# Up-projection of a split-precision feed-forward stage: two of the three products merged into one 512-column product

## The chip, the core and the metric

One core of a Trainium2 chip. The metric is the device time of one execution in microseconds, the median of several. The kernel computes a whole four-layer network in one launch.

## The reference

The network has two transformer layers (differential attention, then latent attention), each followed by the same convolution-gated feed-forward and a per-layer embedding, then two more mixers. Width is 1024, sequence 256, all in float32. What the change touches is this, once per layer of the first two:

```python
def conv_gated_ffn(h, w_in, conv_w, conv_b, w_out):      # h: 256 x 1024, w_in: 1024 x 5632, w_out: 2816 x 1024
    u = h @ w_in                                         # the up-projection
    u_pad = jnp.pad(u, ((0, 0), (CONV_WIDTH - 1, 0), (0, 0)))
    c = conv_b
    for j in range(CONV_WIDTH):                          # 3 taps along the sequence
        c = c + u_pad[:, j:j + s, :] * conv_w[j]
    a, g = jnp.split(c, 2, axis=-1)
    return (jax.nn.silu(g) * a) @ w_out
```

`h` is RMS-normalised first; its gain is folded into `x`, and the row factor 1/rms is applied when the product leaves PSUM.

## The kernel before

**Precision.** Every float32 operand of a product is split in two fp32r parts, high and low. `mm3` (L412 to L415) makes three products of one weight tile: high weight by high x (L413), high weight by low x (L414), low weight by high x (L415), all summed in the same PSUM bank. In the feed-forward the weight tile of 128x128 is the stationary operand and x, 256 tokens wide, streams past it.

**The weight stream.** All weights come as 295 panels of eight 128x128 tiles, in the order of use. SyncE loads a panel into one of six RAW buffers (L380) once its previous content was split. ScalarE (ACT) writes the high part WH (`split_hi`, L1817), which waits until TensorE (PE) has used the panel three before (`w_used`); VectorE (DVE) writes the low part WL (`split_lo`, L1123) after it. There are three WH/WL slots. PE waits for both parts (`take`, L408).

**One feed-forward stage** (`ffn(layer)` on PE L760, DVE L1452, ACT L2006, GpSimd L2420) has 66 panels and 22 hidden tiles j. Hidden tile j has 128 channels of a and 128 of g. Its turn on PE: `hidden` (L765), two panels, eight weight tiles each (one per 128 features of x), a into columns 0 to 255 of a PSUM bank G0 or G1 and g into columns 256 to 511; the banks alternate with j. Then `down` (L776), one panel: the finished hidden tile j-2 times w_out, summed over all j in the four banks A0 to A3. Tile 0 is special (L786 to L795): it goes to a G bank and A3, and its last two k wait for the last parts of x; after it come four small products for the sum of squares (`row_stats`), then tile 1, and turns 2 to 21; at the end two more `down` panels for hidden tiles 20 and 21. After some turns PE makes modulator products for later (L547).

**Around a turn**, the other engines run in a written-out order:
- DVE (`turn`, L1488): split_lo of the next turn's first panel; the eviction `tile` (L1466, one 128x512 operation that multiplies both halves by the row factor, writes U and frees the bank); split_lo; `conv` (two taps, L1473 and L1478, four operations); split_lo.
- ACT (`turn`, L2036): split_hi, split_hi, `conv` (third tap and bias, L2021, two operations, reads U), split_hi, `gate` (Silu, L2027).
- GpSimd (`hidden`, L2423): product of the gated halves twice (L2428, L2429) and its low part (L2432), which lets `down` run.

The panel splits of a turn wait, by w_used, for the panel in the same place of the turn before: the third for `down` of the current turn. ACT's order at the start (L2009 to L2034): splits, `root` of the row sum (L1827), split, split, conv(0), gate(0), split, conv(1), gate(1). DVE's (L1481 to L1486): reciprocal of the row factor (L1138), splits, then tile, split and conv for tiles 0 and 1. In layer 1 DVE also has a second reciprocal in turn 2 and four operations of another branch (L1436) in each of turns 3 and 4, and in both layers one low part for the embedding (L1501) after turn 5.

`UNITS` (L58) counts how often G0 and G1 are evicted in all; the wait counts for a bank come from it (u0).

## Time and profile before

| | us |
|---|---|
| median of 3 executions | 1317.41 (1317.01 to 1320.32) |
| the profiled execution's own time | 1318.33 |
| its span, first to last instruction | 1316.6 |
| mean granted TensorE clock | 0.997 |
| feed-forward stage of layer 0, in the span | from about 173 to 378 |
| feed-forward stage of layer 1 | from about 593 to 798 |

The profile is one execution as the hardware profiler recorded it. PE is TensorE's matmuls, PEld its weight loads, DVE VectorE, ACT ScalarE, POOL GpSimd. In a timeline a row has start and length of an instruction in us; [0.91 <-DVE WL L1123] says that the engine sat idle 0.91 us until DVE's instruction of line 1123 on WL was done; x2 says that two like instructions were merged. Tile names are those of the underlying buffers: U is in ATT, the convolution's result in ATT and HSQ, the gate's in HRS. A matmul's length holds its latency, so the pitch between starts is what it costs.

### The profile page before, as it was taken

Reading aid. Unit: us, or ns where it says so; the run is one execution under the profiler, and the core shown is the slowest. Engines: PE = TensorE matmul, PEld = TensorE weight load, DVE = VectorE, ACT = ScalarE, POOL = GpSimd, SP = SyncE. Lnnn points to the kernel's source line nnn. Section 1 sums busy time; section 2 is a strip of 40 time slices with the busy share of each in tenths; the row PEclk is TensorE's granted clock in tenths of the full one; section 3 lists DMA queues with packets and bytes.
Section 4 is the critical chain, followed back from the end, with each engine's and each line's share of the span. In section 5 each row is a group of like instructions: output and inputs, shape, how many; then the busy total and the mean of one; then the engine's idle time right before and its main releaser. Section 6 shows DMA issues by size and latency. Waiting matters only on the chain.

```text
span 1316.6 us, 24170 instructions
## 1 busy us (share of the span) xinstructions
PE 1259.6 (96%) x8884; PEld 1089.8 (83%) x8884; DVE 883.2 (67%) x1388; ACT 689.6 (52%) x1217; POOL 364.9 (28%) x377
## 2 busy tenths in 40 slices
PE   6999999999999999999999999999989999999996
PEld 4887899999998877898999998888755699987666
DVE  6878588666768985558976667753377548453674
ACT  5555455444567777545554447544367515413562
POOL 4942145344321140144444332011012220000022
PEclk9999999999999999999999999999999999999998
DMA  8565247566545532255665664422200364522100
GB/s 311 178 219 193 65 144 263 202 237 237 198 144 175 165 124 96 67 190 173 228 227 208 236 206 135 134 73 95 95 1 1 71 170 144 160 97 80 49 1 33
DMA packets 50361, 191.72 MB, mean 146 GB/s; under 512 B 5792, under 2 KB 6048, under 8 KB 47968
## 3 DMA queue, kind: packets, MB, share of 16 engines
q1 hardware_dynamic: 43488, 158.59, 36.5%
q0 software_dynamic: 6064, 31.33, 6.8%
q8 instruction: 62, 1.02, 0.3%
q10 hardware_dynamic: 720, 0.57, 0.2%
q14 instruction: 27, 0.22, 0.1%
HBM read 189.41 MB, written 1.05 MB: 145 GB/s over the span
## 4 chain that ended last, share of the span: by engine, by line
PE 78%; DVE 9%; ACT 7%; issue 3%; DMA 1%; POOL 1%; SPq 0%; DVEq 0%; ACTq 0%; POOLq 0%
PE G L413 14%; PE G L415 13%; PE G L414 13%; PE A L413 6%; PE A L415 6%; PE A L414 6%; DVE WL L1123 3%; PE R L633 3%; PE R L559 2%; ACT WH L1817 2%; PE A L991 1%; PE R L413 1%; PE R L415 1%; PE R L414 1%; PE G L1000 1%
## 5 line engine op out<-in xcount | busy, mean ns | idle before, releaser
L1123 DVE TENSOR_TENSOR WL<-RAW,WH 128x1024 fp32r<-128x1024 f32 x295 | 382.2, 1302 | 291.8 <-ACT WH L1817 291.4
L1817 ACT ACTIVATE WH<-RAW 128x1024 fp32r<-128x1024 f32 x295 | 310.4, 1057 | 415.1 <-PE G L415 302.7
L413 PE MATMUL G<-XH,WH 128*128 128x256 f32 (+1 forms) x1336 | 400.1, 299 | 9.6 <-DVE WL L1123 6.3
L414 PE MATMUL G<-XL,WH 128*128 128x256 f32 (+1 forms) x1336 | 394.9, 296 | 0.0
L415 PE MATMUL G<-XH,WL 128*128 128x256 f32 (+1 forms) x1336 | 394.9, 296 | 0.0
L413 PEld LDWEIGHTS G<-XH,WH 128*128 128x128 f32 x1336 | 255.3, 191 | 33.2 <-issue 25.8
L414 PEld LDWEIGHTS G<-XL,WH 128*128 128x128 f32 x1336 | 255.5, 191 | 6.3
L415 PEld LDWEIGHTS G<-XH,WL 128*128 128x128 f32 x1336 | 255.5, 191 | 6.3
L413 PE MATMUL A<-HH,WH 128*128 128x256 f32 x352 | 99.8, 283 | 3.7 <-POOL HL L2432 3.7
L414 PE MATMUL A<-HL,WH 128*128 128x256 f32 x352 | 99.6, 283 | 0.0
L415 PE MATMUL A<-HH,WL 128*128 128x256 f32 x352 | 99.5, 283 | 0.0
L2408 POOL CAST XH<-HRS 128x256 fp32r<-128x256 f32 x24 | 11.4, 474 | 267.3 <-DVE HRS L1714 267.3
L1204 DVE TENSOR_REDUCE SM<-A 128x2 f32<-128x1024 f32 (+1 forms) x80 | 67.8, 849 | 17.9 <-PE A L991 12.9
L413 PEld LDWEIGHTS A<-HH,WH 128*128 128x128 f32 x352 | 67.6, 192 | 4.1 <-ACT WH L1817 4.1
L2428 POOL TENSOR_TENSOR HRS<-HSQ,HRS 128x256 f32<-128x256 f32 x22 | 32.0, 1456 | 128.6 <-ACT HRS L2027 128.6
L415 PEld LDWEIGHTS A<-HH,WL 128*128 128x128 f32 x352 | 67.6, 192 | 0.0
L414 PEld LDWEIGHTS A<-HL,WH 128*128 128x128 f32 x352 | 67.6, 192 | 0.0
L1856 ACT ACTIVATE ATT<-R 128x1024 f32<-128x1024 f32 (+3 forms) x56 | 37.7, 674 | 56.9 <-PE R L633 56.9
L413 PE MATMUL G<-WH,XH 128*128 128x512 f32 (+1 forms) x136 | 54.8, 403 | 12.5 <-DVE XL L1149 11.1
L2428 POOL TENSOR_TENSOR HRS<-ATT,HRS 128x256 f32<-128x256 f32 x22 | 32.1, 1457 | 98.1 <-ACT HRS L2027 92.6
L413 PE MATMUL A<-WH,XH 128*128 128x512 f32 x144 | 57.3, 398 | 1.5 <-DVE XL L1444 1.3
L415 PE MATMUL A<-WH,XL 128*128 128x512 f32 x144 | 56.2, 390 | 0.0
(345 smaller groups left out, 2364.7 us busy)
## 6 DMA issues: line engine op xcount, KB each, us to landing
RAW<-in_wst SPq DMA_DIRECT2D x295, 512.0 KB, 3.8
M<-in_wmod POOLq DMA_DIRECT2D x16, 1024.0 KB, 6.6
M<-in_wmod POOLq DMA_DIRECT2D x16, 512.0 KB, 6.3
B<-in_rpb POOLq DMA_DIRECT2D x4, 1024.0 KB, 12.0
H<-in_x_t SPq DMA_DIRECT2D x2, 512.0 KB, 8.3
M<-in_x_tok SPq DMA_DIRECT2D x1, 1024.0 KB, 13.4
M<-in_ctx_t POOLq DMA_DIRECT2D x1, 1024.0 KB, 5.1
out_y<-M SPq DMA_DIRECT2D x2, 384.0 KB, 2.7
```

Of the source, the lines that this page charges most:

```text
L413: mm(out, lh, rh, start=start, stop=False, skip_group_check=True)
L414: mm(out, lh, rl, start=False, stop=False, skip_group_check=True)
L415: return mm(out, ll, rh, start=False, stop=stop, skip_group_check=True)
L559: m = mm(O[32 * g:32 * g + 32, q * P:(q + 1) * P], SC[:, k, :], RN[:, i % RMS, k * P:(k + 1) * P], start=(k == 0), stop=(k == KD - 1), ski ...
L633: m = nc.tensor.transpose(ST[c][:, k * P:(k + 1) * P], PRB[a % 3][:, c, k * P:(k + 1) * P], IDT)
L991: m = mm(out[c][:, 0:nk * P], Q2[64 * c:64 * c + 64, t, qt * P:(qt + 1) * P], K2[64 * c:64 * c + 64, t // 4, k0:512], start=True, stop=Tru ...
L1000: m = mm(out[64 * c:64 * c + 64, 0:T], V2[:, k + (0 if nk == 4 else 2), kv * 64:(kv + 1) * 64], pt[:, c, k, :], start=(k == 0), stop=(k == ...
L1123: v.tensor_tensor(WL[:, slot, :], RAW[:, raw, :], WH[:, slot, :].bitcast(F32), ALU.subtract).then_inc(w_lo, 1)
L1204: v.tensor_reduce(small(80, a, 2), sc, AX, ALU.max, negate=True).then_inc(at_mx, 1)
L1817: act(WH[:, slot, :], RAW[:, raw, :], ACT.Copy).then_inc(w_hi, 1)
L1856: act(att(s, j)[:, 0:width, 0:nk, q * P:(q + 1) * P], RO[:, :].rearrange("p (l k q) -> p l k q", l=2, k=4)[:, 0:width, 0:nk, :], ACT.Copy) ...
L2428: g.tensor_tensor(HID[b], CB[b][:, 0, :], SG[b], ALU.mult).then_inc(f_hid, 1)
```

## The change

The up-projection makes two products of a weight tile instead of three. XH and XL become halves of one buffer XX, and the high weight tile multiplies both in one product of 512 columns: columns 0 to 255 of the bank get high weight by high x, 256 to 511 high weight by low x. The low weight tile by high x is added to columns 0 to 255. So a bank now holds one of a and g, and the two halves have to be added when it is evicted. ACT copies the right half to LO (in HSQ), DVE adds the left half to it into U, and when both a and g are there DVE multiplies U by the row factor in place. Tile j uses G0 for a and G1 for g; tile 0 uses A2 and A3. `down` and all other stages keep three products.

The order on ACT in a turn becomes: split_hi, copy of a's low half, gate of the tile before, split_hi, copy of g's low half, split_hi, conv. On DVE: split_lo, add a, split_lo, add g, scale, split_lo, conv. At the start ACT has: splits, two copies for tile 0, root, split, split, conv(0), gate(0), two copies for tile 1, split, conv(1). The last gate comes after the loop.

```diff
 
-UNITS = [("l0_o", 4), ("ffn0", 22), ("pp0", 4), ("pg0", 4),
-         ("l1_o", 4), ("ffn1", 22), ("pp1", 4), ("pg1", 4),
+UNITS = [("l0_o", 4), ("ffn0", 42), ("pp0", 4), ("pg0", 4),
+         ("l1_o", 4), ("ffn1", 42), ("pp1", 4), ("pg1", 4),
          ("a_z", 8), ("a_o", 8),
...
         WL = sb("WL", [P, SPL, PW], F32R)
-        XH = sb("XH", [P, 16, T], F32R)
-        XL = sb("XL", [P, 16, T], F32R)
+        XX = sb("XX", [P, 2, 16, T], F32R)
+        XH, XL = XX[:, 0, :, :], XX[:, 1, :, :]
         H = sb("H", [P, KD, T])
...
         CB = [UB[:, 1032:1544].rearrange("p (a t) -> p a t", a=2), HSQ[:, 0, :].rearrange("p (a t) -> p a t", a=2)]
+        LO = HSQ[:, 1, :].rearrange("p (a t) -> p a t", a=2)
         SG = [HRS[:, 0, 0:T], HRS[:, 1, 0:T]]
...
         f_zero, bias_ok = sem("f_zero"), sem("bias_ok")
+        f_low, f_sum, f_u = sem("f_low"), sem("f_sum"), sem("f_u")
         p_hi, p_lo, p_sg, p_m = sem("p_hi"), sem("p_lo"), sem("p_sg"), sem("p_m")
...
 
-                def hidden(par, pslot, bslot, free, p):
+                def both(out, wh, wl, k):
+                    mm(out.rearrange("p (a t) -> p a t", a=2), wh, XX[:, :, k, :], start=(k == 0), stop=False, skip_group_check=True)
+                    return mm(out[:, 0:T], wl, XH[:, k, :], start=False, stop=(k == KD - 1), skip_group_check=True)
+                def hidden(pslot, free, p):
 
-                    pe.wait_ge(bank_free[bslot], free)
                     for c in range(2):
+                        pe.wait_ge(bank_free[c], free)
                         take(p + c)
...
                             wh, wl = wtile((pslot + c) % SPL, k)
-                            m = mm3(G[bslot][:, c * T:(c + 1) * T], wh, wl, XH[:, k, :], XL[:, k, :],
-                                    k == 0, k == KD - 1)
+                            m = both(G[c][:, :], wh, wl, k)
                         m.then_inc(w_used, 1)
...
 
-                pe.wait_ge(bank_free[u0 % 2], u0 // 2)
                 for ks in (range(6), range(6, KD)):
...
                             wh, wl = wtile((p0 + c) % SPL, k)
-                            m = mm3((A[3] if c else G[u0 % 2])[:, 0:T], wh, wl, XH[:, k, :], XL[:, k, :], k == 0, k == KD - 1)
+                            m = both(A[2 + c], wh, wl, k)
                         if k == KD - 1:
...
                 row_stats(tag)
-                hidden(1, p0 + 2, (u0 + 1) % 2, (u0 + 1) // 2, p0 + 2)
+                hidden(p0 + 2, u0 // 2, p0 + 2)
                 def tile(j, i=0):
...
                     q = p0 + 4 + 3 * (j - 2)
-                    hidden(j % 2, q, (u0 + j) % 2, i * 2 + (u0 + j) // 2, i * 12 + q)
+                    hidden(q, i * 4 + (u0 // 2 + j - 1), i * 12 + q)
                     down(j % 2, q + 2, i * 4 + (hb + j - 1), i * 12 + (q + 2), j == 2, False)
...
 
-                def tile(b, bslot, j, p, n):
+                def added(b, c, n):
 
-                    dv.wait_ge(w_used, p)
-                    if isinstance(j, int) and j == 0:
-                        v.tensor_tensor(U[b][:, 0, 2:2 + T], G[bslot][:, 0:T], RST[:, 0, :], ALU.mult)
-                        v.tensor_tensor(U[b][:, 1, 2:2 + T], A[3][:, 0:T], RST[:, 0, :], ALU.mult).then_inc(bank_free[bslot], 1)
-                        return
-                    v.tensor_tensor(U[b][:, :, 2:2 + T], G[bslot][:, :].rearrange("p (a t) -> p a t", a=2),
-                                    bc(RST[:, 0, :], 2), ALU.mult).then_inc(bank_free[bslot], 1)
+                    dv.wait_ge(f_low, 2 * n + c + 1)
+                    v.tensor_tensor(U[b][:, c, 2:2 + T], G[c][:, 0:T], LO[:, c, :], ALU.add).then_inc(bank_free[c], 1)
+                def scaled_by(b, freed):
+                    for c in range(2):
+                        dv.wait_ge(bank_free[c], freed)
+                    v.tensor_tensor(U[b][:, :, 2:2 + T], U[b][:, :, 2:2 + T], bc(RST[:, 0, :], 2), ALU.mult).then_inc(f_u, 1)
 
...
                 ahead(p0 + 2)
-                for j in range(2):
-                    tile(j, (u0 + j) % 2, j, p0 + 2 * j + 2, hb + j)
-                    ahead(p0 + 3 + j)
-                    conv(j, j, hb + j)
+                for c in range(2):
+                    dv.wait_ge(f_low, 2 * hb + c + 1)
+                    v.tensor_tensor(U[0][:, c, 2:2 + T], A[2 + c][:, 0:T], LO[:, c, :], ALU.add).then_inc(f_sum, 1)
+                dv.wait_ge(f_sum, 2 * layer + 2)
+                v.tensor_tensor(U[0][:, :, 2:2 + T], U[0][:, :, 2:2 + T], bc(RST[:, 0, :], 2), ALU.mult).then_inc(f_u, 1)
+                ahead(p0 + 3)
+                conv(0, 0, hb)
+                for c in range(2):
+                    added(1, c, hb + 1)
+                scaled_by(1, u0 // 2 + 1)
+                ahead(p0 + 4)
+                conv(1, 1, hb + 1)
 
-                def turn(b, bslot, j, p, s, r, n):
+                def turn(b, freed, j, p, s, r, n):
 
                     split_lo(p + 3, s % SPL, (r + 0) % RAWS)
-                    tile(b, bslot, j, p + 2, n)
+                    added(b, 0, n)
                     split_lo(p + 4, (s + 1) % SPL, (r + 1) % RAWS)
-                    conv(b, j, n)
+                    added(b, 1, n)
+                    scaled_by(b, freed)
                     split_lo(p + 5, (s + 2) % SPL, (r + 2) % RAWS)
+                    conv(b, j, n)
 
...
                     p = p0 + 4 + 3 * (j - 2)
-                    turn(j % 2, (u0 + j) % 2, j, p, p + 3, p + 3, hb + j)
+                    turn(j % 2, u0 // 2 + j, j, p, p + 3, p + 3, hb + j)
                     if j == 5:
...
                         p = p0 + 16 + 3 * d
-                        turn(d % 2, (u0 + d) % 2, i * 4 + (6 + d), i * 12 + p, p + 3, p + 3, i * 4 + (hb + 6 + d))
+                        turn(d % 2, i * 4 + (u0 // 2 + 6 + d), i * 4 + (6 + d), i * 12 + p, p + 3, p + 3, i * 4 + (hb + 6 + d))
                 nxt[0] = p0 + 67
...
                 p0, u0, hb = START[tag], U0[tag], FT * layer
+                def low(c, bank, p):
+                    ac.wait_ge(w_used, p)
+                    act(LO[:, c, :], bank[:, T:2 * T], ACT.Copy).then_inc(f_low, 1)
                 ahead(p0 + 1)
+                for c in range(2):
+                    low(c, A[2 + c], p0 + c + 1)
                 root(tag, 0, D)
...
 
-                def conv(b, bslot, freed, j, n):
+                def conv(b, j, n):
 
-                    ac.wait_ge(bank_free[bslot], freed)
+                    ac.wait_ge(f_u, n + 1)
                     if not isinstance(n, int) or n >= 2:
...
                 ahead(p0 + 3)
-                conv(0, u0 % 2, u0 // 2 + 1, 0, hb)
+                conv(0, 0, hb)
                 gate(0, hb)
+                for c in range(2):
+                    low(c, G[c], p0 + 3 + c)
                 ahead(p0 + 4)
-                conv(1, (u0 + 1) % 2, (u0 + 1) // 2 + 1, 1, hb + 1)
-                gate(1, hb + 1)
+                conv(1, 1, hb + 1)
 
-                def turn(b, bslot, freed, j, p, s, lands, n):
+                def turn(b, j, p, s, lands, n):
                     split_hi(p + 3, s % SPL, s % RAWS, lands[0])
+                    low(0, G[0], p + 1)
+                    gate(1 - b, n - 1)
                     split_hi(p + 4, (s + 1) % SPL, (s + 1) % RAWS, lands[1])
-                    conv(b, bslot, freed, j, n)
+                    low(1, G[1], p + 2)
                     split_hi(p + 5, (s + 2) % SPL, (s + 2) % RAWS, lands[2])
-                    gate(b, n)
+                    conv(b, j, n)
 
...
                     p = p0 + 4 + 3 * (j - 2)
-                    turn(j % 2, (u0 + j) % 2, (u0 + j) // 2 + 1, j, p, p + 3, lands(p), hb + j)
+                    turn(j % 2, j, p, p + 3, lands(p), hb + j)
                     if j == 4:
...
                         p = p0 + 16 + 3 * d
-                        turn(d % 2, (u0 + d) % 2, i * 2 + ((u0 + 6 + d) // 2 + 1), i * 4 + (6 + d), i * 12 + p, p + 3,
-                             [i * 32 + x for x in lands(p)], i * 4 + (hb + 6 + d))
+                        turn(d % 2, i * 4 + (6 + d), i * 12 + p, p + 3, [i * 32 + x for x in lands(p)], i * 4 + (hb + 6 + d))
+                gate(1, hb + FT - 1)
                 nxt[0] = p0 + 67
```

## Rows read from the trace of the kernel before

**Rows 1.** The page, busy time, share of the span and instructions of each engine.

```profile
PE 1259.6 (96%) x8884; PEld 1089.8 (83%) x8884; DVE 883.2 (67%) x1388; ACT 689.6 (52%) x1217; POOL 364.9 (28%) x377
```

**Rows 2.** The page, chain that ended last, by engine.

```profile
PE 78%; DVE 9%; ACT 7%; issue 3%; DMA 1%; POOL 1%; SPq 0%; DVEq 0%; ACTq 0%; POOLq 0%
```

**Rows 3.** Timeline of PE, layer 0: start us, us, engine, line, operation, out<-in.

```profile
290.39 0.28 PE L413 MATMUL G<-XH,WH 128*128 128x256 f32 x1
...
291.83 0.28 PE L413 MATMUL G<-XH,WH 128*128 128x256 f32 x1
```

**Rows 4.** Timeline of PE, a stage with 512-column products.

```profile
1049.80 0.39 PE L413 MATMUL G<-XH,WH 128*128 128x512 f32 x1
...
1051.84 0.39 PE L413 MATMUL G<-XH,WH 128*128 128x512 f32 x1
```

**Rows 5.** Timeline of PE, start of layer 0's feed-forward stage.

```profile
184.74 0.36 PE L413 MATMUL G<-XH,WH 128*128 128x256 f32 x1 [0.91 <-DVE WL L1123]
...
197.04 0.36 PE L413 MATMUL G<-XH,WH 128*128 128x256 f32 x1 [0.56 <-DVE WL L1123]
```

**Rows 6.** Timeline of PE, last down-projection of layer 0.

```profile
375.60 0.36 PE L413 MATMUL A<-HH,WH 128*128 128x256 f32 x1 [1.86 <-POOL HL L2432]
```

**Rows 7.** Groups of instructions by line and form: xcount | busy us, mean ns | idle.

```profile
L1123 DVE TENSOR_TENSOR WL<-RAW,WH 128x1024 fp32r<-128x1024 f32 x295 | 382.2, 1302 | 291.8 <-ACT WH L1817 291.4
...
L1856 ACT ACTIVATE ATT<-R 128x256 f32<-128x256 f32 x16 | 6.2, 386 | 13.0 <-PE R L633 13.0
...
L1528 DVE TENSOR_TENSOR ATP<-ATP,B 128x512 f32<-128x512 f32 x8 | 5.5, 686 | 1.4 <-ACT ATP L2102 1.4
...
L1168 DVE TENSOR_TENSOR ATP<-R,CS 128x256 f32<-128x256 f32 x9 | 3.4, 415 | 0.0
```

**Rows 8.** Timeline of DVE, start of layer 0's stage.

```profile
183.37 2.36 DVE L1123 TENSOR_TENSOR WL<-RAW,WH 128x1024 fp32r<-128x1024 f32 x2
...
186.31 1.22 DVE L1123 TENSOR_TENSOR WL<-RAW,WH 128x1024 fp32r<-128x1024 f32 x1
187.55 0.88 DVE L1473 SCALAR_TENSOR_TENSOR ATT<-ATT,V 128x256 f32<-128x256 f32 x2
```

**Rows 9.** Timeline of ACT, start of layer 0's stage.

```profile
186.43 1.09 ACT L2021 ACTIVATE ATT<-ATT,V 128x256 f32<-128x256 f32 x2 [1.45 <-DVE ATT L1464]
187.54 1.28 ACT L2027 ACT_TABLE_LOAD   x1
188.99 0.42 ACT L2027 ACTIVATE HRS<-ATT 128x256 f32<-128x256 f32 x1 [0.17 <-DVE ATT L1478]
```

**Rows 10.** Timeline of DVE, two turns of layer 1 apart.

```profile
632.40 1.21 DVE L1123 TENSOR_TENSOR WL<-RAW,WH 128x1024 fp32r<-128x1024 f32 x1
...
641.28 1.21 DVE L1123 TENSOR_TENSOR WL<-RAW,WH 128x1024 fp32r<-128x1024 f32 x1
```

**Rows 11.** Timeline of ACT, end of layer 0's stage.

```profile
370.90 1.06 ACT L1817 ACTIVATE WH<-RAW 128x1024 fp32r<-128x1024 f32 x1 [0.84 <-PE A L415]
371.87 0.40 ACT L2027 ACTIVATE HRS<-HSQ 128x256 f32<-128x256 f32 x1
```

**Rows 12.** Timeline of POOL, last hidden tile of layer 0.

```profile
372.40 1.48 POOL L2428 TENSOR_TENSOR HRS<-HSQ,HRS 128x256 f32<-128x256 f32 x1 [6.74 <-ACT HRS L2027]
...
374.73 0.73 POOL L2432 TENSOR_TENSOR HL<-HRS,HH 128x256 fp32r<-128x256 f32 x1
```

**Rows 13.** Timeline of POOL, first hidden tile of layer 0.

```profile
191.09 1.54 POOL L2432 TENSOR_TENSOR HL<-HRS,HH 128x256 fp32r<-128x256 f32 x1
```

**Rows 14.** Timeline of PE at the kernel's two ends; granted clock after it (PEclk).

```profile
11.10 0.77 PE L413 MATMUL G<-WH,XH 128*128 128x512 f32 x1 [11.10 <-DVE XL L1149]
...
15.08 0.63 PE L413 MATMUL G<-WH,XH 128*128 128x512 f32 x1
...
1307.04 0.70 PE L468 MATMUL R<-ATP,C 128*128 128x256 f32 x2 [0.59 <-ACT ATP L2327]
...
1309.00:1310.00 1.00, 0.00 (x0) 0.66 0.00 0
```

More of the change, by code:

```diff
@@ L1482, in ffn @@
                 ahead(p0 + 2)
-                for j in range(2):
-                    tile(j, (u0 + j) % 2, j, p0 + 2 * j + 2, hb + j)
-                    ahead(p0 + 3 + j)
-                    conv(j, j, hb + j)
-                def turn(b, bslot, j, p, s, r, n):
+                for c in range(2):
[11 more added lines that the diff above has]
+                def turn(b, freed, j, p, s, r, n):
                     split_lo(p + 3, s % SPL, (r + 0) % RAWS)
-                    tile(b, bslot, j, p + 2, n)
+                    added(b, 0, n)
                     split_lo(p + 4, (s + 1) % SPL, (r + 1) % RAWS)
+                    added(b, 1, n)
+                    scaled_by(b, freed)
+                    split_lo(p + 5, (s + 2) % SPL, (r + 2) % RAWS)
                     conv(b, j, n)
-                    split_lo(p + 5, (s + 2) % SPL, (r + 2) % RAWS)
                 for j in range(2, 6):
                     p = p0 + 4 + 3 * (j - 2)
-                    turn(j % 2, (u0 + j) % 2, j, p, p + 3, p + 3, hb + j)
+                    turn(j % 2, u0 // 2 + j, j, p, p + 3, p + 3, hb + j)
                     if j == 5:
```

## The prediction, made before the changed kernel ran

> **What bounds the kernel now.** I read the page first. TensorE is busy for nearly the whole span and VectorE for two thirds of it [rows 1], and the chain that ended last runs mostly through PE, with little in DVE and ACT [rows 2]. Work taken off PE counts in full, unless something else then comes late. The change touches only the two feed-forward stages, some 205 us each (two up-projection panels and one down-projection panel per hidden tile, 22 tiles per layer), so I read the timeline there.
>
> In the middle of a stage PE never waits. A matmul of 256 columns starts every 0.120 us: twelve steps take 1.44 us [rows 3]. A weight tile of three such products costs 0.360 us, a panel of eight 2.88, a turn (two panels up, one down) 8.64. The 512-column products of another stage start every 0.227 us: nine steps take 2.04 us [rows 4]. At 2.4 GHz the columns alone would take 0.107 and 0.213 us, so each matmul carries 0.0133 us that doesn't depend on its width.
>
> The ends of a stage are different. At its start PE waits 0.91 us for a panel's low part and later 0.56 us [rows 5]; at its end it waits 1.86 us for the last hidden tile [rows 6]. There PE hangs on a chain through ACT, DVE and POOL, and the change lengthens that chain.
>
> **PE's own saving.** Columns stay the same (512 + 256 against 3 x 256), one matmul per weight tile goes. An up-projection tile costs 0.2267 + 0.120 = 0.3467 us, a panel 2.77, a turn 8.43 instead of 8.64: 0.213 saved per turn. Over 44 turns, 704 matmuls x 0.0133 = 9.4 us, if nothing else moved. The Trainium skill (TensorE: Matmul & The Clock Gate, "Back-to-back issue gap") gives 2.5 ns beyond the columns for a warm matmul in isolation; by that the saving would be 1.8 us and the sum below 7.6 us higher. The rows show 13.3 ns in streams with a weight load before each matmul, so I keep the rows' value.
>
> **What the evictions cost.** The low half can't be added to the high half in one DVE instruction as cheaply as before: ACT copies each low half (0.39 us for 128x256 from PSUM, two per tile), DVE adds each half (0.42 each), then scales 128x512 (0.69) as the old eviction did [rows 7]. In the steady turn this is covered. Bank G0 is full 2.77 us into a turn and wanted again at 8.43. Between lie PE's signal (0.2), the panel split ahead of the copy on ACT (1.06), the copy (0.4), and on DVE the split (1.3 [rows 7]) and the add (0.4): free at about 6.2, so 2.2 us to spare. DVE's own work per turn is 3 x 1.3 + 0.84 + 0.69 + 1.76 for four convolution steps (0.88 for two [rows 8]) = 7.2 us, against 8.43. Cover is thinner than before but holds. The root of the row sum now stands behind two copies on ACT, about 0.25 us at each start. DMA queues: SP's waits are on the low splits, which come at most one add later, with six raw buffers ahead, so nothing. POOL's modulation loads wait on PE as before: nothing.
>
> **The start of a stage.** Before, tiles alternated banks; tile 2 found its bank long empty. Now tile 2 needs both banks of tile 1, and their low halves are copied on ACT only after the gate of tile 0. I follow layer 0:
> - Root 0.25 later, so the reciprocal and the two splits at 183.37 [rows 8] move to 183.6. PE resumes the second half of tile 1 at 184.95 instead of 184.74 and is ready for tile 2 at 187.8.
> - DVE ends the splits at 185.9 (183.37 + 2.36 = 185.7 before). Two adds with a pitch of 0.35 and a scale that waits for them end at 187.4. ACT's convolution, 186.43 before, starts there [rows 9]; it ends at 188.5, the table load at 189.9. DVE's split (186.31 before) ends 188.5, its convolution gives the gate its input at 189.95.
> - Gate 189.95 to 190.35 (188.99 before), copy to 190.7, add to 191.15, G0 free: PE starts tile 2 at 191.2 instead of 187.8, a hole of 3.4 us.
> - Tile 3 starts at 191.27 + 8.43 = 199.7, where it was 197.04 [rows 5]. The 0.56 us wait there goes, since panels come early now. Term: +2.65.
>
> **The middle.** Tiles 3 to 20 save 18 x 0.213 = -3.85. In layer 1 DVE carries four more operations in each of two turns, a second reciprocal and one longer split near them: its turns then take 8.88 us with no idle (632.40 to 641.28) [rows 10], and with two adds more about 9.6, against PE's 8.43. Starting 2.2 us ahead, less what the reciprocal took, DVE falls behind: tiles 5 and 6 wait for bank 0 about 1.8 us together. Ends: 0 if the slack holds it, 3.0 if splits meet POOL each time.
>
> **The end of a stage.** Before, the last tile's convolution on ACT stood ahead of the third split; now it stands behind it, and that split waits for the down-projection of the same turn. In layer 0's frame (turn 21 starts at 362.0, that is 8.64 and a signal of 0.24 ahead of the split at 370.90 [rows 11]), that split begins at 370.7, ACT convolution ends 372.7, DVE gives the gate its input at 374.2, gate to 374.7 (before 371.87 to 372.27). POOL follows at 374.8 instead of 372.40. Its three operations took until 375.46, 3.06 us, the first 1.48 because DVE was at work [rows 12]; now DVE is idle then and it should take 0.75, but a later split falls beside the others, and one of them took 1.54 beside a split [rows 13]. So 2.3 to 3.2 us: PE's last down-projection starts at 377.2 to 378.1 instead of 375.60. Term +1.6 to +2.5, I take +2.05, in the middle. PE's hole is 3.7 to 4.6 us.
>
> **Sum without the clock.** Layer 0: 2.65 - 3.85 + 2.05 = +0.85. Layer 1: +0.85 + 1.8 = +2.65. Together +3.5 us; ends +0.8 and +5.6.
>
> **The clock.** The four holes (3.4, 3.4 and twice some 4 us) are longer than any idle of PE in the stages before. After PE's last instruction (from 1307.04, 0.70 us long) the granted clock fell between 1309 and 1310, under 3 us later, to its lower level of 1.2 GHz [rows 14]. At the kernel's start PE idled 11.10 us, and at 15.08 a 512-column matmul still took 0.63 us, 0.39 later [rows 4, 14]: some 4.5 us of work at about half speed, which cost 2.25. So a hole costs 0 if the clock stays and about 2.25 if it falls. The row nearest to a hole (the idle end) says it can fall, nothing says it falls each time: I take half, 1.1 each, +4.5 in all; ends 0 and +9. The Trainium skill, same page, "Why this matters for your kernels", says that idle gaps of this kind between bursts bring the low clock back; by it the sum would lie near the upper end.
>
> The forecast: +3.5 + 4.5 = +8.0. The profiled execution took 1318.33 (span 1316.6), which lies 0.92 above the median, so it would go to 1326.3, and the median 1317.41 to **1325.4 us**.
>
> **The rivals.**
> - The clock holds through all holes: +3.5, 1320.9 (1318.2 to 1323.0). For it: PE idled 1.86 us at the stage's end with no fall. Against: the fall after the last instruction.
> - DVE becomes the bound in every turn. If the splits met POOL each time (about 1.65 us instead of 1.3 [rows 13]), DVE's turn would be 8.2, and with waits between its steps up to 8.9; above 8.43 it decides. 36 turns x 0.45 = 16 more: about 1337. Against: DVE sat idle for 291.8 us in all before its splits [rows 7].
> - Faster: the holes don't open, because bank 0 comes free within 1 us of PE's wish and the last convolution isn't held. That leaves nearly -9.4: 1308. Against: the program order of gate, copies and third split is fixed.
> - The change doesn't do what it says: the wide product, whose two halves now lie 4096 elements apart, costs as much as two of 256 columns. No saving: +3.5 + 9.4 + 4.5, 1335. Against: the wide products of another stage, also in two pieces, run at 0.227.
>
> **How the numbers follow.** Forecast (clock falls in some of the holes) 0.52, clock holds 0.28, DVE bound 0.09, no saving from the wide product 0.06, faster 0.05. The range takes in the low bound of the second case and the high bound of the first (+5.6 + 9.0): 1318.5 to 1332. About 0.3% (4 us) is what a measurement can tell from no change. Of the second case 0.17 falls within that, 0.11 above it. Slower: 0.52 + 0.11 + 0.09 + 0.06 = 0.78; same 0.17; faster 0.05.
>
> **What would show it.** Wide matmuls every 0.227 us in the up-projection; a PE wait of 3.4 us for the add of bank 0 ahead of tile 2 in both layers; waits of about 4 us for POOL before the last down-projection; two waits for the bank in layer 1's tiles 5 and 6; the granted clock under 1 in the slices after the holes. Turns of 8.43 us elsewhere. I'm wrong if PE starts tile 2 by 189, if a steady turn is longer than 8.5, or if the matmul pitch differs.

## The result: slower by 1%, and the profile after

| | before | after |
|---|---|---|
| median of the executions timed in turn, us | 1318.24 | 1332.68 (1331.36 to 1333.53) |
| ratio, 95% interval | | 1.0106 [1.0094, 1.0119] |
| span of the profiled execution, us | 1316.6 | 1330.9 |
| mean granted TensorE clock | 0.997 | 0.992 |
| layer 0, first row-sum product of the stage's start to that after its end | 179.9 to 390.1, 210.2 | 179.1 to 394.9, 215.8 |
| layer 1, the same | 599.8 to 809.9, 210.1 | 604.7 to 824.5, 219.8 |

The forecast was +8.0 us, with a range that ended at 1332; measured were +14.4 and 1332.68. The sign and the places were right, the size was not. All of it lies in the two feed-forward stages: +5.6 in layer 0, +9.7 in layer 1. (These add up to 15.3, since the profiled execution of after reached its first stage 0.8 us earlier.) Between and behind the stages nothing moved.

The page of after, busy time by engine:

```profile
PE 1261.6 (95%) x8180; PEld 1057.5 (79%) x8180; DVE 914.2 (69%) x1474; ACT 715.8 (54%) x1305; POOL 362.0 (27%) x377
```

TensorE issues 704 matmuls fewer than in [rows 1] and is busy for 2.0 us more. Holes are idle time, so they can't explain this: the matmuls themselves took longer than foreseen, by their pitch (the time from one start to the next) or by the clock. Next, who made PE wait (total, times, longest):

```profile
PE A L415 <- POOL HL L2459: 9.8, 2, 4.9
...
PE G L769 <- DVE ATT L1468: 4.7, 3, 3.2
...
PE G L769 <- issue: 3.2, 1, 3.2
```

These are four holes and two shorter waits; the "issue" line is the hole of layer 0, which the profile puts down to nothing. That it is a wait for the same bank as in layer 1 is shown by run 4 below, which removes both. In the timeline of PE (start, length, engine, line, operation, idle before and releaser):

```profile
190.09 0.47 PE L769 MATMUL G<-XX,WH 128*128 128x512 f32 x1 [3.21 <-issue]
...
198.69 0.40 PE L769 MATMUL G<-XX,WH 128*128 128x512 f32 x1
...
207.22 0.40 PE L769 MATMUL G<-XX,WH 128*128 128x512 f32 x1
...
378.13 0.55 PE L415 MATMUL A<-HH,WH 128*128 128x256 f32 x1 [4.92 <-POOL HL L2459]
...
382.75 0.41 PE L415 MATMUL A<-HH,WH 128*128 128x256 f32 x1
382.97 0.41 PE L416 MATMUL A<-HL,WH 128*128 128x256 f32 x1
...
615.67 0.79 PE L769 MATMUL G<-XX,WH 128*128 128x512 f32 x1 [3.16 <-DVE ATT L1468]
...
643.45 0.50 PE L769 MATMUL G<-XX,WH 128*128 128x512 f32 x1 [0.53 <-DVE ATT L1468]
...
653.27 0.50 PE L769 MATMUL G<-XX,WH 128*128 128x512 f32 x1 [1.03 <-DVE ATT L1468]
...
807.35 0.55 PE L415 MATMUL A<-HH,WH 128*128 128x256 f32 x1 [4.91 <-POOL HL L2459]
```

What to see: 3.2 us ahead of tile 2 in both layers; 4.9 us ahead of the last down-projection where [rows 6] had 1.86; tiles 5 and 6 of layer 1 waiting for the bank; a turn of 207.22 - 198.69 = 8.53 us with no wait in it, not 8.43. At 382.75 two matmuls of 256 columns stand 0.22 apart instead of 0.12: the clock. In the next rows each number with (x...) is an engine's busy share of that microsecond, in the order PE, PEld, DVE, ACT, POOL; the number right behind them is the granted clock:

```profile
189.00:190.00 1.00, 0.00 (x0) 0.00 (x0) 0.64 (x3) 1.00 (x4) 0.66 (x1) 1.00 0.67 193
190.00:191.00 1.00, 0.91 (x5) 0.85 (x6) 0.90 (x2) 0.75 (x1) 0.86 (x3) 1.00 0.55 221
...
376.00:377.00 1.00, 0.00 (x0) 0.00 (x0) 1.00 (x1) 0.00 (x0) 0.86 (x2) 0.73 0.11 45
377.00:378.00 1.00, 0.00 (x0) 0.00 (x0) 0.41 (x1) 0.00 (x0) 0.99 (x1) 0.50 0.03 8
...
382.00:383.00 1.00, 1.00 (x7) 1.00 (x7) 0.00 (x0) 0.00 (x0) 0.00 (x0) 0.50 0.00 0
383.00:384.00 1.00, 1.00 (x9) 1.00 (x9) 0.44 (x1) 0.38 (x1) 0.00 (x0) 0.85 0.00 0
...
615.00:616.00 1.00, 0.33 (x1) 0.33 (x2) 0.75 (x2) 1.00 (x3) 1.00 (x2) 0.70 0.87 295
616.00:617.00 1.00, 1.00 (x4) 0.81 (x4) 0.95 (x2) 0.39 (x2) 0.86 (x2) 0.50 0.32 131
```

The clock fell to its lower level (0.50) inside both holes of 4.9 us and in the 3.2 us hole of layer 1, not in that of layer 0. The last down-projection of layer 0 ran at that level nearly to its end: 378.13 to 383.36 is 5.23 us for 24 matmuls that take 2.9 at full clock, 2.33 more.

### The profile page after: what moved, and what is told of

Read it like the earlier page. It is cut to its first block, busy times and chain, and to the rows that moved or that the text cites. A ratio compares the mean times of both kernels' runs of the same rounds, so it can differ in the third digit from the quotient of the medians.

```text
span 1330.9 us, 22994 instructions
## 1 busy us (share of the span) xinstructions
PE 1261.6 (95%) x8180; PEld 1057.5 (79%) x8180; DVE 914.2 (69%) x1474; ACT 715.8 (54%) x1305; POOL 362.0 (27%) x377
## 4 chain that ended last, share of the span: by engine, by line
PE 78%; DVE 9%; ACT 7%; issue 3%; POOL 1%; DMA 1%; SPq 0%; DVEq 0%; ACTq 0%; POOLq 0%
PE G L769 11%; PE G L415 8%; PE G L417 8%; PE G L416 8%; PE A L415 6%; PE A L417 6%; PE A L416 6%; PE G L770 5%; DVE WL L1129 3%; PE R L635 3%; PE R L561 2%; ACT WH L1834 2%; PE R L415 1%; PE R L417 1%; PE R L416 1%
## 5 line engine op out<-in xcount | busy, mean ns | idle before, releaser
L769 PE MATMUL G<-XX,WH 128*128 128x512 f32 x672 | 243.0, 404 | 9.8 <-DVE ATT L1468 4.7
L415 PE MATMUL G<-XX,WH 128*128 128x256 f32 (+1 forms) x648 | 202.7, 313 | 4.4 <-DVE WL L1129 3.3
L416 PE MATMUL G<-XX,WH 128*128 128x256 f32 (+1 forms) x648 | 200.5, 309 | 0.0
L417 PE MATMUL G<-XX,WL 128*128 128x256 f32 (+1 forms) x648 | 200.4, 309 | 0.0
L770 PE MATMUL G<-XX,WL 128*128 128x256 f32 x672 | 189.2, 282 | 0.0
L769 PEld LDWEIGHTS G<-XX,WH 128*128 128x128 f32 x672 | 127.0, 189 | 54.4 <-issue 19.4
L415 PEld LDWEIGHTS G<-XX,WH 128*128 128x128 f32 x648 | 123.9, 191 | 12.9 <-issue 5.5
L416 PEld LDWEIGHTS G<-XX,WH 128*128 128x128 f32 x648 | 123.8, 191 | 6.3
L417 PEld LDWEIGHTS G<-XX,WL 128*128 128x128 f32 x648 | 123.7, 191 | 6.2
L770 PEld LDWEIGHTS G<-XX,WL 128*128 128x128 f32 x672 | 127.7, 190 | 0.1
L2435 POOL CAST XX<-HRS 128x256 fp32r<-128x256 f32 x24 | 11.4, 473 | 267.3 <-DVE HRS L1731 267.3
L415 PE MATMUL G<-WH,XX 128*128 128x512 f32 (+1 forms) x136 | 54.7, 402 | 12.3 <-DVE XX L1155 10.4
```

What stands on the lines that cost most here:

```text
L415: mm(out, lh, rh, start=start, stop=False, skip_group_check=True)
L416: mm(out, lh, rl, start=False, stop=False, skip_group_check=True)
L417: return mm(out, ll, rh, start=False, stop=stop, skip_group_check=True)
L769: mm(out.rearrange("p (a t) -> p a t", a=2), wh, XX[:, :, k, :], start=(k == 0), stop=False, skip_group_check=True)
L770: return mm(out[:, 0:T], wl, XH[:, k, :], start=False, stop=(k == KD - 1), skip_group_check=True)
L2435: g.tensor_copy(xh, TMP[m % 2]).then_inc(at_oh, 1)
```

## The experiments

All are edits of the changed kernel, but for one of the kernel before. Percentages are against the kernel before, timed in turn, with their 95% interval; "less" is against the changed kernel unless another run is named. Differences of one or two microseconds between two edited kernels are smaller than these intervals, so there the rows of the traces decide. "..." in a diff or in rows marks what is left out.

**1. Is the pair slower because of where the parts of x lie?** In a turn of after, a wide and a narrow product together took 0.3535 us (averages over both stages: 0.236 from a wide one's start to the next, 0.1175 from a narrow one's), where 0.227 + 0.120 = 0.347 was predicted.

```diff
-        XX = sb("XX", [P, 2, 16, T], F32R)
-        XH, XL = XX[:, 0, :, :], XX[:, 1, :, :]
+        XX = sb("XX", [P, 16, 2, T], F32R)
+        XH, XL = XX[:, :, 0, :], XX[:, :, 1, :]
...
-                    mm(out.rearrange("p (a t) -> p a t", a=2), wh, XX[:, :, k, :], start=(k == 0), stop=False, skip_group_check=True)
+                    mm(out.rearrange("p (a t) -> p a t", a=2), wh, XX[:, k, :, :], start=(k == 0), stop=False, skip_group_check=True)
...
```

> The changed kernel with its x buffer laid out so that the high and low part of one k lie side by side, so the wide product reads 512 adjacent columns; the older 512-column stage now reads pieces 4096 elements apart instead of 2048. Theory A (the distance of the two pieces makes the wide product slow): the wide plus narrow pair in the up-projection drops from 0.352 us to 0.347, 704 x 0.0055 = 3.9 us less, so about 1329; and the older 512-column stage rises from 0.227 us per matmul. Rival B (a narrow product next to a wide one costs extra, wherever the data lie): the pair stays at 0.352 and the time within 1 us of the changed kernel's 1332.7. Both: PE's holes of 3.2 and 4.9 us stay.

Measured 1332.85 (+1.03% [0.88, 1.17]); the pair 0.2356 + 0.1182 = 0.354. The older 512-column stage, whose pieces now lie 4096 apart instead of 2048, kept its 0.227. Placement isn't it.

**2. The same question from the other side**: the parts in two pieces, 4160 instead of 4096 elements apart.

```diff
-        XX = sb("XX", [P, 2, 16, T], F32R)
+        XX = sb("XX", [P, 8320], F32R)[:, :].rearrange("p (a m) -> p a m", a=2)
...
```

> The changed kernel with 64 unused elements behind each half of the x buffer, so the two pieces of the wide product lie 4160 elements apart instead of 4096; nothing else. If the distance being a power of two makes the pair slow, it drops from 0.352 to 0.347 us. If two separate pieces cost extra next to a narrow product at any distance, it stays at 0.352. PE's holes stay.

The pair stayed at 0.2360 + 0.1176 (1332.97, a single execution). Both say that the loss is not in the distance of the two pieces.

**3. Wide products of a panel first, then its narrow ones.**

```diff
                         for k in range(KD):
-                            wh, wl = wtile((pslot + c) % SPL, k)
-                            m = both(G[c][:, :], wh, wl, k)
+                            wide(G[c][:, :], wtile((pslot + c) % SPL, k)[0], k)
+                        for k in range(KD):
+                            wl = wtile((pslot + c) % SPL, k)[1]
+                            m = narrow(G[c][:, :], wl, k)
...
```

> The changed kernel, with each up-projection panel's products in another order: first the eight 512-column products (high weights with both parts of x), then the eight 256-column ones (low weights). Same products, same sums, same evictions. Theory A (the 13.3 ns per dropped product are partly lost because wide and narrow products alternate; a pair takes 0.3535 us there where 0.227 + 0.120 = 0.347 was predicted): with one change of width per panel instead of fifteen, the pair falls to about 0.347, a turn from 8.53 to 8.43, 704 x 0.0065 = 4.6 us less, time about 1328. The holes at both ends of a stage stay (3.2 and 4.9 us). Theory B (the loss has to do with the weights or with the operands, whatever the order): the pair stays 0.3535 and the time 1332.7.

Measured 1331.46 (+0.98% [0.83, 1.14]), 1.2 less than after. PE's timeline in the first turns (the second row is the end of the first, read by itself):

```profile
199.95 2.00 PE L769 MATMUL G<-XX,WH 128*128 128x512 f32 x8
201.11 0.84 PE L769 MATMUL G<-XX,WH 128*128 128x512 f32 x3
201.79 1.11 PE L773 MATMUL G<-XX,WL 128*128 128x256 f32 x8
202.74 2.00 PE L769 MATMUL G<-XX,WH 128*128 128x512 f32 x8
...
208.42 0.86 PE L769 MATMUL G<-XX,WH 128*128 128x512 f32 x3
```

Eight wide products take 1.84 us (0.230 each), eight narrow 0.95 (0.119), and the turn 208.42 - 199.95 = 8.47 instead of 8.53. So alternation costs 0.06 per turn, 2.6 us over 44. But in this run the clock fell in all four holes (it was 0.50 from 190 to 193 too), about 1.7 us that after didn't pay: the time hides the gain. Run 8 repeats it with the clock held.

Read one by one, the eight wide products from 199.95 on take 0.233, 0.236, 0.229, 0.232, 0.231, 0.227, 0.226 and 0.227 us: the first five behind a change of width are longer, the last three have the pitch of the all-wide stream. The next panels show the same. Five longer ones cost 0.028 us, the first narrow one (0.113 instead of 0.120) gives back 0.007: 0.02 per panel, 0.04 per turn. It isn't the place k in x either: where wide and narrow alternate, the pitches repeat every three pairs, while k runs to eight.

**4. Other banks at the stage's start**: tile 0 goes to G0 and G1, tile 1 to A2 and A3, so tile 2 waits for tile 0's adds and not for tile 1's. PE now has to wait for tile 1's adds ahead of the first down-projection, which writes A2 and A3.

```diff
-                            m = both(A[2 + c], wh, wl, k)
+                            m = both(G[c][:, :], wh, wl, k)
...
-                hidden(p0 + 2, u0 // 2, p0 + 2)
+                hidden(p0 + 2, None, p0 + 2, A[2:4])
...
+                    if j == 2:
+                        pe.wait_ge(f_sum, 2 * layer + 2)
...
```

> The changed kernel with the banks of the first two hidden tiles exchanged: tile 0 in G0 and G1, tile 1 in A2 and A3, so tile 2 finds its banks empty. Theory (the hole ahead of tile 2 is a bank wait on the copies behind the first gate): both 3.2 us holes go, and with them the low clock of 3.4 us in layer 1 that cost about 1.7; a wait of 0.6 us for a panel comes back ahead of tile 3: 1332.7 - 6.4 + 1.2 - 1.7 = about 1325.8. Rival (the lost time at the start is ACT and DVE being busier, so the wait only moves): PE waits as long ahead of tile 2 or 3 for a panel, the time stays above 1330.

Measured 1327.51 (+0.67% [0.54, 0.80]), 5.2 less. PE's waits in it:

```profile
PE A L415 <- POOL HL L2464: 9.8, 2, 4.9
...
PE A L415 <- DVE WL L1134: 1.9, 2, 0.9
PE A L769 <- DVE WL L1134: 1.9, 2, 0.9
```

Both 3.2 us holes are gone, against 0.94 for a panel's low part at tile 2's down-projection, and the clock stayed up there. It is 1.7 us short of the expectation; in layer 1's crowded turns a wait of 1.16 us for a panel's high part stands where after had 0.53. The holes of 4.9 us at the end are untouched: the two ends of a stage have separate causes.

**5. A shorter chain at the stage's end**: copy, add and scale of g ahead of the second split, the convolution ahead of the third, on DVE and on ACT.

```diff
-                    split_lo(p + 4, (s + 1) % SPL, (r + 1) % RAWS)
                     added(b, 1, n)
                     scaled_by(b, freed)
+                    split_lo(p + 4, (s + 1) % SPL, (r + 1) % RAWS)
+                    conv(b, j, n)
                     split_lo(p + 5, (s + 2) % SPL, (r + 2) % RAWS)
-                    conv(b, j, n)
...
```

> The changed kernel with the order in each turn altered: the low half of g is copied ahead of the second split on ACT, both adds and the scale come ahead of the second split on DVE, and the convolution ahead of the third split on both, as before the change. Theory (the 4.9 us hole at the stage's end is the last tile's convolution held behind two splits): the hole shrinks to about 2 us in both layers, the clock doesn't fall there any more (2.3 us each): 1332.7 - 2 x (3.0 + 2.3) = about 1322. Rival (the end's chain is as long through POOL and the added operations whatever the order): hole 4 us or more, time above 1329. A third way: the new order is worse in the steady turn, where PE then waits for bank 0 in every turn, and the time rises above 1333.

Measured 1330.72 (+0.86% [0.73, 0.99]): a miss; the hole (4.2 us) and the time are those of the rival. Its six executions lay between 1327.13 and 1334.16, with mean granted clocks of 0.994 to 0.989; the profiled one was the slowest, with a fall in all four holes. The three POOL operations and PE in its trace:

```profile
376.77 1.53 POOL L2455 TENSOR_TENSOR HRS<-HSQ,HRS 128x256 f32<-128x256 f32 x1 [4.05 <-PE A L417]
...
378.27 1.70 POOL L2456 TENSOR_TENSOR HH<-HSQ,HRS 128x256 fp32r<-128x256 f32 x1
...
380.11 0.72 POOL L2459 TENSOR_TENSOR HL<-HRS,HH 128x256 fp32r<-128x256 f32 x1
380.98 0.36 PE L415 MATMUL A<-HH,WH 128*128 128x256 f32 x1 [4.22 <-POOL HL L2459]
```

The gate came 1.7 us earlier in the turn, but now POOL's work fell together with two DVE splits (376.51 and 377.95): 4.05 us for three operations that would take 2.2 at the 0.73 of after's rows below. Of the 1.7 us that the order gave, 0.7 reached the hole (4.92 to 4.22); the collision took back the rest.

**6. Filler products in the holes**, into a bank that nobody reads (26 ahead of tile 2, 36 ahead of the last down-projection, per layer), to hold the clock up while the holes stay.

```diff
+                filler(26)
...
+                filler(36)
                 down(1, p0 + 65, hb + FT, p0 + 65, False, True)
```

> The changed kernel with products that nobody reads put into PE's holes (26 of 256 columns ahead of hidden tile 2, 36 ahead of the last down-projection, into a bank that is free), so that PE works there but starts the next real product no earlier. Theory (the clock falls because of the holes and costs 1.7 + 2.3 + 2.3 us beyond them): granted clock 1.00 in every slice, last down-projection at 0.120 us per matmul, time 1332.7 - 6 = about 1326.5. Rival (the low clock costs nothing beyond the holes or has another cause): time 1332 or more.

Measured 1326.87 (+0.60% [0.47, 0.73]), as expected. From some 20 us into the kernel to PE's last instruction the granted clock stayed at 1.00. The real product behind the filler starts no earlier in its turn than in after:

```profile
378.82 0.36 PE L415 MATMUL A<-HH,WH 128*128 128x256 f32 x1 [0.62 <-POOL HL L2467]
```

Turn 21 began at 362.21 here, 16.61 us before (in after 361.54 and 378.13, 16.59). So the fallen clock costs 1332.68 - 1326.87 = 5.8 us in after, and the work that the change moved or added costs the other 8.6. Between the two traces the stages differ by 2.2 us in layer 0 and 4.1 in layer 1.

**7. Layout, start and end together.**

> The changed kernel with the three earlier edits together: x parts side by side, banks of tiles 0 and 1 exchanged, the turn's order altered. Theory (three separate causes that add up): the pitch of the pair gives 704 x 0.0055 = 3.9, the start 5.2 as measured alone (1332.7 - 1327.5), the end some 1.4 less wait: 1332.7 - 10.5 = about 1322, with holes of 4.2 us ahead of the last down-projections and a low clock after them. Rival (the causes overlap: DVE, which is a bound of its own, takes back what PE gains): above 1325, with new PE waits in the steady turns.

Measured 1325.46 (+0.54% [0.39, 0.70]), 3.5 above the expectation, which still booked 3.9 us for the layout; run 1 had shown that to be nothing. The start and the order add up without it. The end holes were 3.65 us, and in both the clock fell.

**8. Filler products and the batched order**, to price alternation without the clock.

> The kernel with filler products in the holes (which keeps the clock up all through; it took 1326.87), with wide products ahead of narrow ones in each panel as in the run of that order alone. In that run the records show a wide product every 0.230 and a narrow one every 0.119 us inside a panel, so 0.349 for a pair instead of 0.3535, 704 x 0.0047 = 3.3 us less, but its time fell only 1.2: there the clock also fell in the hole at the start of layer 0, which the changed kernel's did not. Theory: with the clock held up the order is worth its 3.3 us: about 1323.6. Rival (the order is worth only 1.2, and the fall of the clock in layer 0 has nothing to do with it): 1325.7.

Measured 1324.35 (+0.45% [0.31, 0.58]), 2.5 less than run 6, with turns of 8.47 us and no low clock around the holes. The two intervals overlap, but the slowest execution here (1325.46) is faster than run 6's fastest (1326.20), and the turns say the same: the 2.5 is the 0.06 per turn of run 3 (2.6); my 3.3, from averages of starts, was too much. Alternation is shown as a cause, worth 0.06 of the 0.10 us by which a turn missed. The other 0.04 is the longer wide products behind each of the two changes of width that a batched turn keeps, as read in run 3. So, by the rows, the whole 0.10 goes with changes of width; the last 0.04 was read and not removed by an edit, and what in the engine does it stays open.

**9. Work to put in the hole**: the first panel of the next projection (which needs nothing of the last tile) ahead of the last down-projection, its panel moved forward in the stream; with the edits of runs 1 and 4.

```diff
-                down(1, p0 + 65, hb + FT, p0 + 65, False, True)
+                pe.wait_ge(p_hi, layer + 1)
+                pe.wait_ge(p_lo, layer + 1)
+                for u in range(2):
+                    gemm_unit(U0[f"pp{layer}"] + u, p0 + 65, 4 * u, 2, 8, 2)
+                down(1, p0 + 66, hb + FT, p0 + 66, False, True)
...
```

> x parts side by side, banks exchanged, and the first panel of the per-layer embedding's projection moved ahead of the stage's last panel (the two panels change places in the stream), so that PE has 2.9 us of real work in the hole at the stage's end. Theory: both end holes shrink from 4.9 to about 2.0 us and the clock stays up there: against 1332.7, 3.9 for the pitch, 5.2 for the start, 2 x (2.9 + 2.3) for the end: about 1313, faster than the kernel before. Rival (the moved work only shifts the wait, since what follows waits for the same last tile): above 1318.

Measured 1326.23 (+0.61% [0.47, 0.75]), only 1.3 less than run 4 and 13 above the expectation: a miss. 3.9 of that is again the layout. The hole shrank to 2.06, but PE then waits for the sums in H, which used to be there by then:

```profile
377.45 0.36 PE L415 MATMUL A<-HH,WH 128*128 128x256 f32 x1 [2.06 <-POOL HL L2465]
382.66 0.39 PE L415 MATMUL A<-XX,WH 128*128 128x256 f32 x1 [0.78 <-DVE H L1538]
386.07 0.35 PE L415 MATMUL G<-XX,WH 128*128 128x256 f32 x1 [0.28 <-DVE XX L1161]
389.98 0.36 PE L415 MATMUL G<-XX,WH 128*128 128x256 f32 x1 [0.55 <-ACT WH L1840]
```

Also in this one profiled run the clock was low from 23 to 28, behind a hole of 2.17 at a place that no edit touches (run 1 has the same behind 3.17 us), and behind the hole of 2.06 in layer 0, but not behind that of 2.06 in layer 1.

**10. The same with the edit of run 5.**

> The same with the turn's order altered as well. Theory: another 0.7 us per layer off the hole: about 1312. Rival: the order costs as much in contention between DVE's splits and POOL as it gains, as seen where POOL's three operations took 4.1 us: no gain over the one without it.

Measured 1322.11 (+0.29% [0.18, 0.41]), 10 above the expectation (built on run 9's), but 4.1 less than run 9: the rival, no gain, is wrong too. The clock was up throughout, and the holes were 1.40:

```profile
375.94 0.35 PE L415 MATMUL A<-HH,WH 128*128 128x256 f32 x1 [1.40 <-POOL HL L2465]
```

**11. The moved panel in the kernel before**, as a control.

> The kernel before, with the first panel of the next projection (2.88 us of work for TensorE that needs nothing of the last hidden tile) moved ahead of the last down-projection panel. Theory: before, TensorE waits 1.86 us for POOL at the end of each feed-forward stage; both go, 3.7 us, time about 1315. Rival (what follows the stage was hidden behind that wait and comes late instead, as new waits of the kind seen when the same move was made in the changed kernel): 1317 to 1320.

Measured 1320.08 (+0.09% [0.00, 0.18]): no gain.

```profile
380.20 0.39 PE L413 MATMUL A<-XH,WH 128*128 128x256 f32 x1 [0.78 <-DVE H L1516]
383.61 0.36 PE L413 MATMUL G<-XH,WH 128*128 128x256 f32 x1 [0.27 <-DVE XL L1150]
387.52 0.35 PE L413 MATMUL G<-XH,WH 128*128 128x256 f32 x1 [0.55 <-ACT WH L1818]
```

The 1.86 us of [rows 6] went and came back as smaller waits. That hole stood in front of work that DVE and ACT did meanwhile. In the changed kernel runs 7 and 10 differ by the panel move alone: 3.35 us less. In run 7's trace PE worked some 9 us at half clock, which by itself cost about 4.5 (an estimate from those rows), and in run 10's none. So what the move is worth there can be put down to the clock.

**12. All that was borne out, and layer 1's extra work spread**: runs 3, 4, 5 and 9 (without the layout), and of layer 1's eight extra VectorE operations one in every second turn of the loop instead of four in each of two turns.

```diff
-                    elif layer == 1 and j < 5:
-                        modulated_full(0, 1, CX, range(4 * j - 12, 4 * j - 8))
...
+                        if layer == 1 and d % 2:
+                            k = bass.ds(i * 2 + d // 2, 1)
+                            v.scalar_tensor_tensor(XT[1][:, k, :], CX[:, k, :], GS[:, 0, 1, k], RST[:, 1, :].unsqueeze(1),
+                                                   ALU.mult, ALU.mult).then_inc(x_full, 1)
```

> The changed kernel with everything that the experiments bear out: tile 0 in banks 0 and 1 of G and tile 1 in A (no hole ahead of tile 2), last tile's adds, scaling and convolution ahead of the later panel splits, first panel of the next projection ahead of the last down-projection, wide products of a panel ahead of its narrow ones, and layer 1's eight extra VectorE operations spread over the sixteen turns of the loop, one in every second, instead of four in each of two turns. The run with the first three took 1322.1. If alternation costs 4.6 and the crowded turns of layer 1 cost 2 to 3: about 1315, 3 us below the kernel before. If alternation costs nothing: 1319 to 1320. If the spread operations delay other turns instead: 1317 to 1318.

Measured 1317.61 against 1318.78 for the kernel before, timed in turn: ratio 0.9989 [0.9980, 0.9998], some 1.2 us under it and 15.1 under the changed kernel. In layer 1's first turns one wait for the bank is left, where run 10 still had turns of 9.66, 9.75 and 9.74 us; here they are 9.64, 8.58 and 8.47:

```profile
625.68 2.11 PE L769 MATMUL G<-XX,WH 128*128 128x512 f32 x8 [0.45 <-DVE ATT L1480]
```

That is 2.4 us for the spread. With the 2.6 of the order off run 10's 1322.1 that makes 1317.1, near what was measured; the 1315 of the expectation had 4.6 for alternation, and its third case had the right time for a wrong reason, since no other turn got longer. With all of it the kernel is about 0.1% faster than before, below what I called tellable, though these 11 executions put the interval just under 1. Not all of that need be the merged product: spreading layer 1's extra operations wasn't tried on the kernel before.

## Why the prediction was wrong: its steps

| step | predicted, us | measured, us |
|---|---|---|
| middle of a stage, 18 turns | -3.85 | -2.1 |
| start: tile 3 late by | +2.65 (hole 3.4) | +2.5 (hole 3.2) |
| end | +2.05 (hole 3.7 to 4.6) | +2.9 (hole 4.9) |
| layer 1's crowded turns | +1.8 | +2.1 |
| clock, both layers | +4.5 | +5.8 |

The first three rows are for each layer, the others for both together.

**The step that failed: "each matmul carries 0.0133 us that doesn't depend on its width".** It came from an all-wide and an all-narrow stream, and both hold in after. But the changed order alternates, and there is no row of an alternating stream in the trace of before. A turn fell by 8.64 - 8.53 = 0.11 us instead of 0.21, half; over 44 turns 4.4 us of the 9.4 are missing. The rival "no saving from the wide product" put the loss in the two pieces 4096 apart; runs 1 and 2 exclude that, and runs 3 and 8 show alternation in its place for 0.06 of the 0.10, with the other 0.04 behind the changes of width that are left. I gave this term no range at all, which is the real mistake: 704 times a difference of two pitches needs bounds on both sides. The Trainium skill (TensorE: Matmul & The Clock Gate, "Back-to-back issue gap") has 2.5 ns beyond the columns for a warm matmul in isolation. What a dropped matmul gave here, 0.11/16 = 6.9 ns, lies between that and my 13.3.

**The start** was right, chain and size. The rows of after show it as foretold: gate, then the copies, then adds, and PE at 190.09 on the first add's heels (the two start 0.34 apart and the first ends at 189.99).

```profile
188.84 0.42 ACT L2051 ACTIVATE HRS<-ATT 128x256 f32<-128x256 f32 x1 [0.17 <-DVE ATT L1485]
189.16 0.64 ACT L2029 ACTIVATE HSQ<-G 128x256 f32<-128x256 f32 x2
...
189.56 0.76 DVE L1468 TENSOR_TENSOR ATT<-G,HSQ 128x256 f32<-128x256 f32 x2 [0.36 <-ACT HSQ L2029]
```

Copies took 0.32 each where [rows 7] suggested 0.39, and the root, which waits for the row sum anyway, stood no later behind it than before (1.06 us in both traces); hence 3.2 and not 3.4. Run 4 confirms the cause by removing it.

**The end** was right in kind, 0.85 per layer too small, and beyond my upper bound of 2.5. The rows of after, last tile of layer 0:

```profile
370.71 0.69 DVE L1474 TENSOR_TENSOR ATT<-ATT,RST 128x512 f32<-128x512 f32 x1
371.47 1.23 DVE L1129 TENSOR_TENSOR WL<-RAW,WH 128x1024 fp32r<-128x1024 f32 x1
371.58 1.10 ACT L2045 ACTIVATE HSQ<-ATT,V 128x256 f32<-128x256 f32 x2
372.82 0.88 DVE L1480 SCALAR_TENSOR_TENSOR HSQ<-ATT,V,HSQ 128x256 f32<-128x256 f32 x2
373.84 0.88 DVE L1485 SCALAR_TENSOR_TENSOR HSQ<-ATT,V,HSQ 128x256 f32<-128x256 f32 x2
374.36 0.42 ACT L2051 ACTIVATE HRS<-HSQ 128x256 f32<-128x256 f32 x1 [1.68 <-DVE HSQ L1485]
...
374.91 0.73 POOL L2455 TENSOR_TENSOR HRS<-HSQ,HRS 128x256 f32<-128x256 f32 x1 [5.72 <-ACT HRS L2051]
375.60 0.73 POOL L2456 TENSOR_TENSOR HH<-HSQ,HRS 128x256 fp32r<-128x256 f32 x1
375.75 1.65 DVE L1129 TENSOR_TENSOR WL<-RAW,WH 128x1024 fp32r<-128x1024 f32 x1 [1.03 <-ACT WH L1834]
376.47 1.52 POOL L2459 TENSOR_TENSOR HL<-HRS,HH 128x256 fp32r<-128x256 f32 x1
```

The gate came 0.55 us later in the turn than worked out, because I dropped what lies between the steps (0.07, 0.12 and 0.14 us between DVE's rows above, 0.18 before ACT's). POOL took 3.08 us: the later split doubled one of its operations, as I had foreseen, and I took the middle where the upper bound was due.

**The clock**: "a hole costs 0 if the clock stays and about 2.25 if it falls", of which I took half for each of four, was right within 1.3 us in the sum, and that by luck: it fell in three holes of four in this execution, in all four in those profiled in runs 3 and 5. Together 5.8 (run 6), the 2.33 at the end of layer 0 among them. That rival "clock holds" had 0.28 was too kind: 1.86 us without a fall says nothing of 4 us. The Trainium skill, same page ("Why this matters for your kernels"), says that such gaps bring the low clock back; the trace agrees for both holes of 4.9 us and for the one of 3.2 in layer 1, but not for that of 3.2 in layer 0.

**The sum.** Over the two layers, against the steps: middle +3.5, end +1.7, clock +1.3, crowded turns +0.3, start -0.3. That is 6.5 more than +8.0, 14.5, where 14.4 was measured. Half the error is the pitch of the pair. Two signs of being wrong caught it: the matmul pitch (0.236 for a wide product, not 0.227), and "a steady turn is longer than 8.5", by 0.03. The rival "no saving" had 1335, nearer to 1332.68 than my 1325.4; the turns show that this nearness is chance, since half the saving is there. The verdict "slower by over 0.3%", at 0.78, held. Of the rivals, DVE as the bound in every turn didn't come about: layer 1's turns outside the crowded ones took what layer 0's did (8.53, or 8.63 and 9.62 where modulator products stand between).

## What to carry to other kernels

A pitch read in a uniform stream is a price for uniform streams; when an edit mixes widths, bound the saving from below, and if you can, keep products of one width together (here 0.06 us a turn for a reordering of two loops). Giving each tile two banks instead of one, and its eviction more steps, cost nothing in the steady turn here; the banks cost 3.2 us at a stage's start and the longer chain some 3 us at its end. So cost the first and last tile by hand, with the work in between at its real pace. A hole of the size seen here (2 us and more) must be priced with the clock behind it; and an idle gap is worth filling only if what follows it isn't itself waiting on the others.

## What the runs showed of the hardware

- A 512-column and a 256-column product in alternation take 0.3535 us a pair, in batches of eight 0.349; all-wide and all-narrow streams add up to 0.347. The loss sits in the wide one (0.236, 0.230, 0.227), and in a batch only in the first five behind the narrow ones (0.229 to 0.236, then 0.227; run 3).
- Over these traces PE's holes of 3.2 us at a stage's start dropped the granted clock to 0.50 in seven cases of ten (one of two in after and in runs 1 and 2, both in runs 3 and 5), holes of 3.65 to 4.9 in all fourteen. Of shorter ones, the two of 1.86 in the kernel before and those of 2.10 and 1.40 in run 10 left it up; one of 2.17 and one of the two of 2.06 in run 9 did not. So the length alone doesn't decide it near 2 to 3 us. At that level a 256-column product came every 0.213 us instead of 0.120.
- POOL's 128x256 operations took 0.73 us beside an idle DVE and 1.5 to 1.7 when they started during a panel split, and a split that started during one of them went from 1.23 to 1.65. In these rows the later of the two ended about one undisturbed length behind the end of the earlier: in after POOL's operation at 376.47 met the split of 375.75 to 377.40 and ended at 377.99, 0.59 behind it. Moving work of one of them earlier is worth only what it doesn't push into the other.
- A wait for POOL that ended a stage, 1.86 us in the kernel before, was worth nothing: its removal gave 1.0009 [1.0000, 1.0018].
